# The opening of a two-block fp32 kernel: features taken in halves, matmuls on constants ahead of it, and three residual subtractions on GpSimd

## The reference, cut to what matters

```python
mod = silu(c) @ w_ada + b_ada                  # c: 1 x 1024, w_ada: 1024 x 3072
shift, scale, gate = split(mod, 3)
h = rms_norm(x, norm_g) * (1 + scale) + shift   # 512 x 1024
proj = h @ w_in                                 # q, keys and values, gates, u, z
...
y = s5_mixer(u, a_re, a_im, log_dt, ...)        # state space layer on the columns u
y = gelu(y)
y = y * sigmoid(y @ glu_w + glu_b)              # gated linear unit
mix = concat([attn * silu(z_a), y * silu(z_s)]) @ w_out
x = x + gate * mix
```

## Time and profile before

| | us |
|---|---|
| median of three runs (906.15 to 906.69) | 906.59 |
| the profiled execution's own time | 905.98 |
| its span on the core | 904.2 |
| TensorE busy | 875.7 (97%) |
| VectorE busy | 578.9 (64%) |
| ScalarE busy | 450.7 (50%) |
| GpSimd busy | 99.7 (11%) |

### The profile page before, as it was taken

How to read it: one execution, slowest core, us unless ns; L and a number is a source line. 1 busy time by engine, 2 the same in 40 slices (tenths; PEclk the granted TensorE clock), 3 DMA queues, 4 the chain that set the end, 5 groups by cost and what they waited for, 6 DMA issues and landing times.

```text
span 904.2 us, 14652 instructions
## 1 busy us (share of the span) xinstructions
PE 875.7 (97%) x5733; PEld 708.0 (78%) x5733; DVE 578.9 (64%) x1154; ACT 450.7 (50%) x956; POOL 99.7 (11%) x121
## 2 busy tenths in 40 slices
PE   3999999999999999999999999999999999999996
PEld 1579888784677778788888888888888888888885
DVE  5899797989888564666465455345476556445533
ACT  4734323386787334465535466234366554555531
POOL 1001112012400000000010232000000001131202
PEclk9999999999999999999999999999999999999998
DMA  9836655347200313323223424122322332342203
GB/s 384 335 98 140 176 159 168 125 133 240 94 2 2 116 62 118 118 88 95 71 94 116 141 94 131 51 94 94 120 88 67 94 106 96 125 140 71 84 10 94
DMA packets 34678, 104.69 MB, mean 116 GB/s; under 512 B 14961, under 2 KB 14961, under 8 KB 32178
## 3 DMA queue, kind: packets, MB, share of 16 engines
q1 hardware_dynamic: 28098, 85.77, 28.5%
q0 software_dynamic: 3856, 15.73, 5.5%
q10 hardware_dynamic: 2656, 2.26, 1.0%
HBM read 98.37 MB, written 4.19 MB: 113 GB/s over the span
## 4 chain that ended last, share of the span: by engine, by line
PE 92%; DVE 4%; ACT 2%; DMA 1%; issue 1%; SPq 0%; POOL 0%; POOLq 0%; ACTq 0%; DVEq 0%
PE bank L1101 85%; PE bank L1461 2%; PE bank L1615 2%; PE bank L1441 2%; DMA ring<-in_w_ada 1%; PE bank L1501 1%; DVE arena L1749 1%; PE bank L1491 0%; ACT arena L768 0%; DVE xn_t L2271 0%; DVE ring_lo L2295 0%; DVE w_lo L2243 0%; ACT soft L861 0%; DVE pw L1743 0%; DVE x_t L2331 0%
## 5 line engine op out<-in xcount | busy, mean ns | idle before, releaser
L2243 DVE TENSOR_TENSOR w_lo<-ring,w_hi 128x1024 fp32r<-128x1024 f32 x80 | 101.4, 1270 | 51.8 <-ACT w_hi L943 49.3
L1101 PE MATMUL bank<-hT_hi,w_hi 128*128 128x512 f32 x320 | 129.4, 404 | 0.0
L1101 PE MATMUL bank<-hT_lo,w_hi 128*128 128x512 f32 x320 | 125.2, 391 | 0.0
L1101 PE MATMUL bank<-hT_hi,w_lo 128*128 128x512 f32 x320 | 124.9, 390 | 0.0
L1101 PE MATMUL bank<-w_hi,hT_hi 128*128 128x512 f32 x256 | 101.7, 397 | 0.3 <-DVE hT_lo L2289 0.3
L1101 PE MATMUL bank<-w_lo,hT_hi 128*128 128x512 f32 x256 | 99.9, 390 | 0.0
L1101 PE MATMUL bank<-w_hi,hT_lo 128*128 128x512 f32 x256 | 99.8, 390 | 0.0
L943 ACT ACTIVATE w_hi<-ring 128x1024 fp32r<-128x1024 f32 x80 | 84.3, 1057 | 14.0 <-PE bank L1101 13.8
L1101 PEld LDWEIGHTS bank<-hT_hi,w_hi 128*128 128x128 f32 x320 | 60.1, 188 | 16.8 <-issue 4.7
L1101 PEld LDWEIGHTS bank<-hT_lo,w_hi 128*128 128x128 f32 x320 | 60.1, 188 | 13.1
L1101 PEld LDWEIGHTS bank<-hT_hi,w_lo 128*128 128x128 f32 x320 | 60.2, 188 | 11.2
(11 more groups left out here) (341 smaller groups left out, 1834.3 us busy)
## 6 DMA issues: line engine op xcount, KB each, us to landing
ring<-in_w_units SPq DMA_DIRECT2D x80, 512.0 KB, 3.7
ring<-in_w_ada SPq DMA_DIRECT2D x4, 2048.0 KB, 10.3
bias_ring<-in_na_bias POOLq DMA_DIRECT2D x6, 1024.0 KB, 5.2
ring<-in_w_out SPq DMA_DIRECT2D x2, 2048.0 KB, 8.8
bias_ring<-in_t_bias POOLq DMA_DIRECT2D x8, 448.0 KB, 3.7
x_t<-in_x SPq DMA_DIRECT2D x4, 512.0 KB, 5.7
arena<-in_w_ada SPq DMA_DIRECT2D x1, 2048.0 KB, 19.9
arena<-in_w_ada SPq DMA_DIRECT2D x2, 1024.0 KB, 22.8
```

What stands on the lines that cost most here:

```text
L1101: return pe.matmul(out, lhsT, rhs, start=first, stop=last)
L2243: dve.tensor_tensor(w_lo[:, u % 4], raw_w[:, u % 4], w_hi[:, u % 4].bitcast(fp32), SUB).then_inc(S["w_split"], 1)
```

## The change

- **Order of the loads**: w_ada 0 goes into the arena, w_ada 2 into `cl`, then w_u, then w_ada 1 into slot 1, then (when TensorE has used w_ada 0) w_ada 3 in two halves into the arena, the tables, then w_k, which waits until w_ada 1 is used.
- **TensorE** first runs five matmuls of constants (identity times 512 columns, full fp32) as soon as the constants are in. Then: piece 0, tile 0, columns 0, tile 1, piece 2, tiles 2 and 3, columns 2. With that, h is known for features 0 to 511 (k = 0 to 3), and half a pass (4 matmuls) of u's pieces is run at a time (`u_pass`); pieces 1 and 3 of w_ada and their columns come in between, and the second halves after them. The first piece of u is now made of three passes like the others.
- **ACT** rounds u's first piece between the copies of tile 1 and tile 2, and takes the sines after the second half of h.
- **DVE** does each half's `modulate` and rests of h when its columns are there; the powers move behind the second half; `part_lo(0)` is new, `part_lo(1)` to `part_lo(3)` go to POOL; `part_lo(12)`, `part_lo(13)` and the dot products move behind the keys' sums of squares.

```diff
+        ADA = [0, 2, 1, 3]
+        ROW_PLACE = [5, 5, 6, 7]
...
         def _(sp):
...
-            for c, parts in enumerate(chunks):
+            sp.dma_start(arena[:, 0:SLOT], ada[0]).then_inc(ada_late_in[0], 16)
+            sp.dma_start(cl[:, 0:SLOT], ada[2]).then_inc(ada_late_in[1], 16)
+            for c in (CH_U, 1, *range(CH_K, len(chunks))):
...
-                if c == SLOTS - 1:
-                    sp.dma_start(arena[:, 0:SLOT], ada[2]).then_inc(ada_late_in[0], 16)
+                if c == 1:
+                    sp.wait_ge(S["ada_done"], 1)
                     for n in range(2):
...
         def _(pool):
...
             inv_root(D, EPS, "x_rstd", lambda v: v[:, 0:NT])
+            for n in range(1, 4):
+                pool.wait_ge(S["p_hi"], n)
+                pool.tensor_tensor(p_lo(n), p_raw(n), p_hi(n).bitcast(fp32), SUB).then_inc(S["p_lo"], 1)
             pool.wait_ge(S["xT_done"], 2 * NT)
...
+            move_rows(0)
+            move_hT(0)
+            move_hT(1)
+            part_hi(0)
+            move_rows(1)
+            move_hT(2)
+            move_hT(3)
+            round_x(0)
+            part_hi(1)
+            part_hi(2)
+            part_hi(3)
+            move_rows(2)
+            move_rows(3)
+            round_x(1)
+            act.wait_ge(S["ang_ready"], 1)
+            act.activation(ang3[:, 0:160], ang[:, 0:160], ACT.Sin).then_inc(S["sin_ready"], 1)
...
+            def u_pass(f, half, which):
+                w, h = ((p_hi, x_hi), (p_lo, x_hi), (p_hi, hT_r))[which]
...
+                for k in range(4 * half, 4 * half + 4):
+                    if f == 0 and which != 1:
+                        pe.wait_ge(S["h_lower" if which else "h_hi"], k + 1)
+                    ins = mm(bank[f][:, :], w(f)[:, k, :], h[:, k, :], which == 0 and k == 0, which == 2 and k == KD - 1)
...
             pe.wait_ge(S["params_in"], 32)
+            for n in range(5):
+                mm(bank[5][:, :], ident, cons[:, 0:512], True, True)
             pe.wait_ge(S["c_silu"], 1)
...
+            pe.wait_ge(ada_late_in[0], 16)
+            times_c(bank[ROW_PLACE[0]], ada_late[0]).then_inc(S["ada_done"], 1)
+            turn_x(0)
+            mod_columns(0)
+            turn_x(1)
+            pe.wait_ge(ada_late_in[1], 16)
+            times_c(bank[ROW_PLACE[1]], ada_late[1]).then_inc(S["ada_done"], 1)
+            turn_x(2)
+            turn_x(3)
+            mod_columns(1).then_inc(S["mod_cols"], 1)
+            for f, which in ((0, 0), (0, 1), (1, 0), (0, 2), (1, 1), (1, 2)):
+                u_pass(f, 0, which)
+            arrived(1)
+            pe.wait_ge(S["xT_evac"], 2 * NT)
+            times_c(bank[ROW_PLACE[2]], slot(1, KD, 512)).then_inc(S["ada_done"], 1)
+            for which in range(3):
+                u_pass(2, 0, which)
+            pe.wait_ge(S["ada_done"], 3)
+            pe.sem_inc(S["w_free"], 2)
+            for n in range(2):
+                pe.wait_ge(ada_late_in[2 + n], 16)
+                ins = times_c(bank[ROW_PLACE[3]], ada_late[0], range(4 * n, 4 * n + 4))
+            ins.then_inc(S["ada_done"], 1)
+            mod_columns(2)
+            u_pass(3, 0, 0)
+            mod_columns(3).then_inc(S["mod_cols"], 1)
+            u_pass(3, 0, 1)
+            u_pass(3, 0, 2)
+            for f, which in ((0, 0), (0, 1), (1, 0), (1, 1), (0, 2), (1, 2), (2, 0), (2, 1), (2, 2), (3, 0), (3, 1), (3, 2)):
+                u_pass(f, 1, which)
...
-            pe.wait_ge(u_ahead[0], 16)
-            for k in range(KD):
-                pe.wait_ge(S["h_raw"], k + 1)
-                ins = mm(bank[0][:, :], p_raw(0)[:, k, :], hT[:, k, :], k == 0, k == KD - 1)
...
-            for f in range(1, 4):
-                proj_T(PT_U + f, f)
...
             less_turns(ang, ang2, C1)
             normal(2)
+            normal(3)
             less_turns(ang, ang2, C2)
-            normal(3)
+            part_lo(0)
             less_turns(ang, ang2, C3)
...
+            modulate(0)
+            lower_x(0)
             within(ang)
...
             ts(r1, em1, 1.0, None, ADD, ALU.bypass)
+            modulate(1)
+            lower_x(1)
             settle(dve.memset(pw_r[:, 0, :], 1.0))
...
+            dve.wait_ge(S["p_lo"], 3)
             part_lo(4)
...
             squares(keys_w, NG, ss3[:, :, 10:12], qtmp).then_inc(S["k_stats"], 1)
+            part_lo(12)
+            part_lo(13)
...
             dve.wait_ge(S["k_rstd"], 1)
```

More of the change, by code:

```diff
@@ L204, in build @@
         mod_rows = soft[:, 0:2 * D]
-        ada_late = [cut(arena[:, n * SLOT:(n + 1) * SLOT], k=KD, n=512) for n in range(2)]
+        ada_late = [cut(v[:, 0:SLOT], k=KD, n=512) for v in (arena, cl)]
+        ADA = [0, 2, 1, 3]
         gate_part = cl[:, 4096:4608]
@@ L669, in _, with move_rows, move_hT @@
             act.activation(th, zr, ACT.Tanh, scale=0.5).then_inc(S["em_ready"], 1)
[L671 to L677, removed]
+            def move_rows(n):
+                act.wait_ge(S["ada_done"], n + 1)
+                act.activation(mod_rows[:, ADA[n] * 512:(ADA[n] + 1) * 512], bank[ROW_PLACE[n]][:, :], ACT.Copy).then_inc(S["mod_row"], 1)
+            def move_hT(i):
                 for b in range(2):
@@ L681, in _ @@
                         .then_inc(S["xT_evac"], 1)
[L682 to L687, removed]
             def proj(p):
@@ new lines, in u_pass @@
+            def u_pass(f, half, which):
+                w, h = ((p_hi, x_hi), (p_lo, x_hi), (p_hi, hT_r))[which]
+                if not half and which < 2:
+                    pe.wait_ge(S[("p_hi" if f else "u0_hi", "p_lo" if f else "u0_lo")[which]], max(f, 1))
+                for k in range(4 * half, 4 * half + 4):
+                    if f == 0 and which != 1:
+                        pe.wait_ge(S["h_lower" if which else "h_hi"], k + 1)
+                    ins = mm(bank[f][:, :], w(f)[:, k, :], h[:, k, :], which == 0 and k == 0, which == 2 and k == KD - 1)
+                if half and which == 2:
+                    ins.then_inc(S["proj_done"], 1)
@@ L1934, in _ @@
             dve.tensor_tensor(cl5[SN:P, :, 0], ca[0:SN], cb[0:SN], SUB).then_inc(S["cl_ready"], 1)
-            part_lo(12)
-            part_lo(13)
[L1938 to L1944, removed]
-            ins.then_inc(S["lam_dot"], 1)
             ss3, rs3 = (cut(v[:, 0:48], i=NT, h=12) for v in (ss, rstd))
@@ L1999, in _ @@
             squares(keys_w, NG, ss3[:, :, 10:12], qtmp).then_inc(S["k_stats"], 1)
+            part_lo(12)
+            part_lo(13)
+            for l in range(LAYERS):
+                sl = slice(l * HD, (l + 1) * HD)
+                for m, (a, b) in enumerate((("lq1", "lk1"), ("lq2", "lk2"))):
+                    ins = dve.tensor_tensor_reduce(kc_sb[:, 0:HD], row(a)[:, sl], row(b)[:, sl], 1.0, 0.0, MUL, ADD,
+                                                   lam_t[:, 2 * l + m:2 * l + m + 1])
+                    if 2 * l + m < 2 * LAYERS - 1:
+                        settle(ins)
+            ins.then_inc(S["lam_dot"], 1)
             dve.wait_ge(S["k_rstd"], 1)
```

138 lines of the change are left out of this document (49 added, 89 removed).

## The result

The changed kernel took 910.36 us, median of 4 runs (909.31 to 912.0), against 906.37 (906.04 to 906.69) for the kernel before on the same chip: a ratio of 1.0045, 95% interval 1.003 to 1.006. It is slower by 4 us where 0.8 had been forecast, and above the range's upper end of 909.8. The profiled execution took 909.31, with a span of 907.5 against 904.2: 3.3 us are to be found in it.

The account below looks back on a forecast made before the run. TensorE, busy 97% of the span, was taken to bound the kernel, with VectorE ending last at the state products. Opening 0 plus lateness 0.8 on 905.98 gave 906.8, and 0.6 for the median 907.4; range 904.0 to 909.8.

Parts of the forecast that it names:

- the removed work: TensorE's opening: half-rate start 1.7 us and u's first piece in three passes 1.3, together 3.0, given back as waits.
- both idle times, 4.2 together: VectorE before `state_ready`: idle times of 3.33 and 0.85 us, filled by moved work, absorb lateness of 6.4, leaving 2.2.
- rival D: u's rests: GpSimd pays for sharing with VectorE, first subtraction 6.5 us, TensorE stands 3.9 more, 911.3; chance 0.04.
- 0.8 had been written: State products: `state_ready` at 131.4, so TensorE goes on at 131.55 instead of 130.75, costing 0.8 us.
- TensorE's opening: Up to the end of u's fourth piece: 57.2 against 57.08 before, counted as 0 in the sum.
- rival B: ScalarE's opening: held up by u's first piece landing at 21.6, everything 1.3 us later, 908.7; chance 0.20.
- carried to 31.9: u's second piece: TensorE waits 0.7 us, until 31.9, for its rest, which needs 2.58 on GpSimd.
- Rival A: Whole kernel: the removed 3.0 us reach the end, 903.6, or with half of them 905.1; chance 0.20.
- Rival C: First `times_c`: the constants fail their purpose, it starts at 15.4 and takes 3.64, 910.0 us; chance 0.06.
- the 6.3 carried: Five products of constants: begin at 6.8 and end near 13.1, 4 us of it at half rate, hidden under w_ada's wait.
- What was costed at nothing: Waits for piece 3 and w_k, ScalarE's sines, GpSimd's later constants, arena placement, and GpSimd beside VectorE: 0, the last at most 0.5.

Follow-up runs that it names:

- late heads: Changed kernel with VectorE's wait for the inverse root and the keys' scaling moved behind the state, ahead of the turning of the keys: 907.41 us, ratio 1.0018.
- gap filled: Changed kernel with two more full products of constants ahead of u's first half pass: 909.48 us, ratio 1.0038.
- u's rests on VectorE: Changed kernel with u's three subtractions back from GpSimd to VectorE, behind the rests of h's first half: 909.69 us, ratio 1.0039.
- the last runs: Changed kernel with keys' scaling late, w_ada 1 sent and multiplied early, u's rests on VectorE: 904.32 us; powers early too: 904.69; without late scaling: 906.08.
- the rests on VectorE and piece 1 early: Changed kernel with u's three subtractions on VectorE and w_ada 1 sent behind u's first part and multiplied in TensorE's gap: 906.08 us, ratio 1.0005.
- the four kernels with piece 1 early: Changed kernel with w_ada 1 sent and multiplied early: alone 908.18 us; with u's rests on VectorE 906.08; also keys' scaling late 904.32; also powers early 904.69.

## Why the prediction was wrong

It had the mechanism: the removed work comes back as waits, and VectorE, late behind h's second half, ends last at the state products. Two terms of the sum were mis-sized.

- **The term that failed first** is that both idle times, 4.2 together, are filled by the two rests and the dot products beside GpSimd's inverse root, which leaves 2.2 of VectorE's lateness. Measured: 4.8 left. The work did go there, but it made GpSimd's two steps 1.75 longer, so 1.84 of the wait stayed; the other 0.75 is that VectorE's stretch started later than carried (51.85 against 51.1). The prediction asked only what GpSimd costs VectorE, and looked for GpSimd paying (rival D) at the subtractions of u alone. The late heads put the price of VectorE at 2.5 us of the products where 0.8 had been written.
- **TensorE's opening**, "57.2 against 57.08", cost nothing in the sum; it cost 1.07. Up to the first columns the steps were right: u's first part was in ScalarE's hands at 20.23 (20.3 assumed, so rival B fell), the columns at 24.40 (24.6). Then the pass on the rest of u's second piece, carried to 31.9, started at 32.30, behind two delays that lie over one another: a half pass of 1.78 instead of 0.93, at a clock that the prediction took for settled once released, and GpSimd's first subtraction, 3.46 instead of 2.58. Without the first it starts at 32.26 (gap filled), without the second at 31.95 (u's rests on VectorE). The second columns came at 44.02 (43.2). So of the 0.95 that u's fourth piece is behind the carried 57.2, 0.4 stands at that pass, 0.4 more by the second columns and 0.1 behind them; the 0.4 in between are not traced to one step.
- **Rival A** (the removed 3.0 reach the end) fell as argued, and the last runs show what it lacked: with the gap used, the rests on VectorE and the heads late, the products start 2.4 earlier than before and the time falls by 1.7, of the 3.0 that were removed.
- **Rival C** fell: the constants save 1.7 in the record and 2.1 in the time. They took 7.42 and not the 6.3 carried, ending at 14.46, just as the piece landed.
- **Rival D** was given 0.04 with one price and one place. GpSimd does pay, at the subtractions far less than the 6.5 written (2.94 to 3.52), and at the inverse root, where VectorE waits for it. The row that the prediction leaned on the earlier trace rows is of an instruction with one tensor as input and so does not show the two-input case that it cited beside it; VectorE's rests (99.73) beside the inverse root do.
- **What was costed at nothing** held: no wait at `cl_ready` (96.92, as against 96.2 carried), none for piece 3.

## What to carry to other kernels

Work moved into an engine's wait is free only if it does not lengthen what that engine waits for: price the waited-for instructions with the moved work beside them. When two stalls cover one another (here a half-rate clock and a late rest), taking away either shows nothing; here it paid only when both were gone and the gap was put to use. Where an engine of 64% busy time ends last, look on it for a wait and work behind it whose result nobody needs yet, and move both back.

## What the runs showed of the hardware

**GpSimd and VectorE wait each other out.** GpSimd's three subtractions in the kernel after took 3.46, 3.52 and 2.94, the last two by these rows:

```profile
32.21 3.52 POOL L553 TENSOR_TENSOR ring_lo<-ring,a_hi 128x1024 fp32r<-128x1024 f32 x1
35.69 2.94 POOL L553 TENSOR_TENSOR ring_lo<-ring,a_hi 128x1024 fp32r<-128x1024 f32 x1
```

Beside them VectorE's three instructions at 30.03, 33.53 and 36.30 took 3.47, 2.84 and 2.44 (their times in the kernel with the rests on VectorE and piece 1 early are 1.39, 0.78 and 0.17). They ended at 33.5, 36.4 and 38.7, where the subtractions ended near 32.2, 35.7 and 38.6: each a little less than its usual length behind one. The subtractions in turn ended some 2.2 behind the end of a VectorE instruction (30.0, 33.5, 36.4), so by these rows an estimate of a subtraction's own length is 2.2, and the rest of it is waiting. At the inverse root the same is seen: GpSimd's step of 0.20 took 1.10 and ended at 101.0, where VectorE's first rest ended at 100.9, and its power, 3.77 instead of 2.92, ended 2.8 behind the second rest (102.1).

The Trainium skill states this in "SBUF — State Buffer", Who interferes with whom: the two engines share a pair of ports as an exclusive lock, which VectorE needs for instructions with two inputs there and in its two-port modes; whichever instruction is first has it to its end, and the other blocks. These rows agree. They don't agree that every GpSimd instruction keeps it to its end: in the kernel with the late heads the copy at 103.94 took its usual 0.69, and VectorE's dot products their usual 0.22 to 0.24, while GpSimd's power on 128x16 was running (101.14 to 104.91).

**The clock can fall again in the middle of an opening.** After TensorE's single-column products and an idle time of 2.08, the granted clock of 24.3 to 32 was 0.78, against 1.00 from 16 to 24.3. All seven profiles with this idle time show it (0.78, once 0.56); with the idle time filled it was 1.00. It cost 0.7 in a half pass (1.78 against 1.09) and 1.6 in a `times_c` (3.48 against 1.92). In the four kernels with piece 1 early TensorE ran the same instructions up to that point and stood idle for 0.87 to 0.90; in the profile of one the clock fell, in the other three it did not.
